# The third block's projections over 528 columns: meta tokens beside the tokens, keys and first values weights-stationary

## Chip, core and metric

The kernel runs on one core of a Trainium2 chip. The metric is device time in microseconds (us) from the start of the program to its end, the median of the runs shown. TensorE's granted clock has two levels, 1.2 and 2.4 GHz; a granted clock of 1.00 is the upper one.

## What is computed

Two blocks of one kind (layers 0 and 1) and then a block of another kind (the third block, `L2` in the code) work on 512 tokens of width 1024. The third block puts 16 learned meta tokens ahead of the 512, so that keys and values have 528 rows, and projects the normalised tokens to two kinds of queries, keys and values. Queries and keys are normalised per head of 64 and rotated:

```python
meta = jnp.broadcast_to(meta_tokens.astype(x.dtype)[None], (bsz, N_META, D_MODEL))
x = jnp.concatenate([meta, x], axis=1)
...
h = rms_norm(x, attn_norm_g[l])
proj = jnp.einsum('bld,de->ble', h, w_in[l])
qa, ka, va, qb, kb, vb = jnp.split(proj, splits, axis=-1)
qa = apply_rope_2(rms_norm(qa.reshape(bsz, length, A_HEADS, HEAD_DIM), a_q_norm_g[l]), ang_a)
ka = apply_rope_2(rms_norm(ka.reshape(bsz, length, A_KV_HEADS, HEAD_DIM), a_k_norm_g[l]), ang_a)
va = va.reshape(bsz, length, A_KV_HEADS, HEAD_DIM)
...
return x[:, N_META:]
```

Attention over `ka`, `va` and the differential attention over `kb`, `vb` follow, then an output projection and a feed-forward part. Only the 512 rows of the tokens are returned, so the meta tokens need keys and values alone, and no queries.

## The kernel before, in words

Activations lie transposed: 128 features to a partition row, `KT` = 8 tiles of features, 512 tokens along the free dimension. Every product of an activation and a weight is done as three matmuls (`product`, line 1759): both operands are split into a high and a low part (`h_hi`, `h_lo`, `w_hi`, `w_lo`), and high x low, low x high and high x high are added up in PSUM. One chunk of weights is 128 x 1024; SyncE (SP) loads the chunks in order into six slots, each when the chunk six places ahead has been used up (`w_used`), and GpSimd (POOL) splits each into its two parts. Nothing schedules the work but the order in which each engine's instructions are written down, and semaphores.

Four places matter here.

The first is `gemm_first` (line 1804). It follows a norm whose output comes in two halves of 256 tokens, eight feature tiles each; VectorE (DVE) finishes a tile of `h_lo` at line 1197 and counts `h_ready`. TensorE takes three chunks (four in the third block) side by side, half by half, and within a half tile by tile: for each feature tile `k` it waits for that tile and then does all chunks. Layer 1 calls it for `ik`, `iq0`, `iq1`, the third block for `qa0` to `qa3`.

The second is the run of key tiles (from line 2252): `ka0`, `kb0` to `kb3`. For each, 24 matmuls stream the 512 tokens through the weights; then `meta_keys` (line 2227) does 24 more with the 16 meta tokens as the stationary operand and the 128 weight columns streamed, into its own PSUM bank; then `head_sums_2` (line 2236) adds up squares of an earlier tile, one full-precision matmul over 512 columns.

The third is the values `va` (from line 2262): tokens are the stationary operand, four blocks of 128 tokens with 24 matmuls of 128 columns each; between the blocks stand two head sums and the five small transposes that turn the meta keys (`kmt`, line 2270); then 24 matmuls for the meta tokens' values (`vam`), the head sum of the meta keys, and at once the first block of `vb` (`values_in(0, ...)`), after which the scores begin (`scores_2`, line 2312 in the rows).

The fourth is the chain beside it. ScalarE (ACT) copies each finished tile from PSUM (`raw2`, line 1062), starts two DMAs that swap neighbouring rows (line 732), squares it (line 1067) and, when TensorE has summed the squares of the tile before, takes that tile's Ln and Exp (lines 752 and 753). DVE does the rotation of each tile in four instructions (`rope_2`, lines 1388 to 1405), using the swapped rows and the result of the Exp. The scores wait for all rotations (`rope_done`). There are 14 rows in this list of tiles, `R2_NAMES`: eight of queries, five of keys, and `mk`, the 80 columns of the meta keys.

Of the kernel before, what the change touches and what calls it, by code (L numbers as in the profile page):

```python
# [16 lines left out]
F32 = mybir.dt.float32  # L17
# [6 lines left out]
P = 128  # L24
D = 1024
T = 512
# [36 lines left out]
TM = T + META  # L63
L2 = LAYERS
GRID = 64
R2_NAMES = ("qa0", "qa1", "qa2", "qa3", "qb0", "qb1", "qb2", "qb3", "ka0", "kb0", "kb1", "kb2", "kb3", "mk")
# [48 lines left out]
def weight_plan():  # L115
# [36 lines left out]
    def second_mixer(l):  # L152
        for i, n in enumerate(R2_NAMES[:-1]):
            chunks.append((l, n))
            tile((l, n), i if i < 4 else (i - 4) % 3)
        tile((l, "mk"), 3)
# [83 lines left out]
def program(nc, wst, xin, pos, cst, vec, cst2, meta, gates, out):  # L240
    chunks, index, ready, bankof, seq, before = weight_plan()
    ctx = ExitStack()
    with ctx:
# [9 lines left out]
        h_hi = sbt("h_hi", 16, KT, T, dt=F32R)  # L253
        h_lo = sbt("h_lo", 32, KT, T, dt=F32R)
        w_raw = [sbt(f"w_raw{i}", 48 + 8 * i, 1024) for i in range(WSLOTS)]
        w_lo = [sbt(f"w_lo{i}", 48 + 8 * i, 1024, dt=F32R) for i in range(WSLOTS)]
        w_hi = [sbt(f"w_hi{i}", 52 + 8 * i, 1024, dt=F32R) for i in range(WSLOTS)]
        cos_t, sin_t = sbt("cos_t", 96, T), sbt("sin_t", 98, T)
        rstd = sbt("rstd", 100, T)
        kc = sbt("kc", 102, C_W)  # L260
        vecs = sbt("vecs", 106.28125, V_W)
        small = sbt("small", 106.625, 128)
        WK = 107.25
# [44 lines left out]
        hm_hi = sbt("hm_hi", WK + 99, KT, META, dt=F32R)  # L308
        hm_lo = sbt("hm_lo", WK + 99.5, KT, META, dt=F32R)
# [4 lines left out]
        raw2 = [sbt(f"raw2{i}", WK + 51 + 2 * i, T) for i in range(TURNS)]  # L314
        rsq2 = [sbt(f"rsq2{i}", WK + 63 + 2 * i, T) for i in range(2)]
        rrs2 = [sbt(f"rrs2{i}", WK + 67 + 2 * i, T) for i in range(2)]
        rt3, rt4 = sbt("rt3", WK + 71, T), sbt("rt4", WK + 73, T)
        rot2 = [sbt(f"rot2{i}", WK + 75 + 2 * i, T) for i in range(TURNS)]
        kmt = sbt("kmt", WK + 87, 5 * P)
# [4 lines left out]
        kept = [sbt(f"kept{i}", 96 + 2 * i, T) for i in range(KEPT)]  # L324
# [8 lines left out]
        def bank(b, lo=0, n=512):  # L333
            return ps[:, 512 * b + lo:512 * b + lo + n]

# [90 lines left out]
        kmt_ready = sem("kmt_ready")  # L426
        mk_ready = sem("mk_ready")
# [185 lines left out]
        def _(eng):  # L613
# [85 lines left out]
            def scaled_top(n, j):  # L699
# [8 lines left out]
                eng.activation(h_hi[:, j, :], x_sb[:, j, :], ACT.Copy, scale=vecs[:, g:g + 1]).then_inc(hi_ready, 1)  # L708
# [38 lines left out]
            def head_norm_2(r):  # L747
                w = 5 * META if R2_NAMES[r] == "mk" else T
                eng.wait_ge(rms_ready, Q0 + r + 1)
                if r >= 2:  # L750
                    eng.wait_ge(rope_done, R0 + r - 1)
                after(step(eng.activation(rrs2[r % 2][:, 0:w], bank(6 + r % 2, 0, w), ACT.Ln, scale=1.0 / AD, bias=eps)))
                eng.activation(rrs2[r % 2][:, 0:w], rrs2[r % 2][:, 0:w], ACT.Exp, scale=-0.5).then_inc(rrs_ready, 1)

            for l in range(LAYERS):
# [207 lines left out]
                def split_y(i):  # L963
# [4 lines left out]
                    eng.activation(h_hi[:, i, :], src, ACT.Copy).then_inc(ysp_hi, 1)  # L968
# [81 lines left out]
            for r in range(len(R2_NAMES)):  # L1050
                n = (L2, R2_NAMES[r])
                w = 5 * META if n[1] == "mk" else T
                if n[1] == "mk":
                    acc(n)
                    eng.activation(kmt[0:META, :], ps[0:META, 3 * 512:3 * 512 + 5 * P], ACT.Copy).then_inc(kmt_ready, 1)
                    eng.wait_ge(mk_ready, 1)
                    a = bank(5)
                else:
                    a = acc(n)
                if r >= TURNS:  # L1060
                    eng.wait_ge(rope_done, R0 + r - TURNS + 1)
                free(eng.activation(raw2[r % TURNS][:, 0:w], a[:, 0:w], ACT.Copy), n)
# [8 lines left out]

            free(eng.activation(va_sb[:, :, :].rearrange("p a b -> p (a b)"), acc((L2, "va")), ACT.Copy), (L2, "va"))
# [43 lines left out]
            def result(u):  # L1116
# [5 lines left out]
                if u < PAIRS_A:  # L1122
                    eng.activation(h_hi[:, u, :], bank(7), ACT.Copy).then_inc(ysp_hi, 1)
# [8 lines left out]
            def kept_split(u):  # L1132
                acc((L2, "vb3"))
                eng.wait_ge(y2_kept, u + 1)
                eng.activation(h_hi[:, u, :], kept[u][:, :], ACT.Copy).then_inc(ysp_hi, 1)
# [6 lines left out]
            def result_split(h):  # L1142
                eng.wait_ge(yb_ready, h + 1)
                eng.activation(h_hi[:, 4 + h, :], osb2[:, :], ACT.Copy).then_inc(ysp_hi, 1)
# [25 lines left out]
        def _(eng):  # L1170
# [63 lines left out]
            def scaled_rest(n, j):  # L1234
                g = V_NORM + 8 * n + j
                eng.wait_ge(hi_ready, tiles_before(n) + j + 1)
                eng.scalar_tensor_tensor(h_lo[:, j, :], x_sb[:, j, :], vecs[:, g:g + 1], h_hi[:, j, :].bitcast(F32),
# [115 lines left out]
            def meta_norm():  # L1353
# [9 lines left out]
                after(step(eng.tensor_copy(hm_hi[:, :, :], sqm[:, :, :])))  # L1363
                eng.tensor_tensor(hm_lo[:, :, :], sqm[:, :, :], hm_hi[:, :, :].bitcast(F32), ALU.subtract)\
# [7 lines left out]
            def rope_2(r):  # L1372
# [1211 lines left out]
```

## Time and profile before

| | us |
|---|---|
| median of three runs | 2254.21 |
| lowest and highest run | 2252.89, 2254.99 |
| span of the profiled execution | 2253.1 |
| TensorE busy | 2230.7 (99%) |
| GpSimd busy | 1484.0 (66%) |
| VectorE busy | 1034.2 (46%) |
| ScalarE busy | 618.9 (27%) |

The profile gives the profiled execution's time as its span alone, from the first to the last instruction. Busy shares are averages over all stages. A matmul's shown duration is longer than its share of the engine, because matmuls overlap; what one costs is the distance from its start to the start of the next. The third block begins near 1594 us of the span, its scores near 1705 us; layer 1 begins near 805 us.

### The profile page before, as it was taken

The page shows a single profiled execution, that of the slowest core. Times are in us where ns is not written, and L with a number is a line of the kernel's source. Part 1 is how long each engine was busy: PE and PEld are TensorE (multiplying, and loading weights), DVE is VectorE, ACT ScalarE, POOL GpSimd, SP SyncE. Part 2 cuts the span into 40 slices and gives each one's busy share as a digit, 9 for nine tenths or more (in the row PEclk, how much of TensorE's full clock was granted, in tenths as well). Part 3 has the DMA queues.
Part 4 walks back from the last instruction along what each step waited for, and adds up shares of the span by engine and source line. Part 5 has one row for each costly group of instructions (what it writes and reads, how often), then busy time and mean ns, then how long its engine had stood idle before and what let it go on. Part 6 is the DMA issues. An engine that isn't in the chain of part 4 may idle for free.

```text
span 2253.1 us, 33380 instructions
## 1 busy us (share of the span) xinstructions
PE 2230.7 (99%) x12339; PEld 1795.8 (80%) x12339; DVE 1034.2 (46%) x1567; ACT 618.9 (27%) x1103; POOL 1484.0 (66%) x1452
## 2 busy tenths in 40 slices
PE   8999999999999999999999999999999999999999
PEld 7777888888888897778788888888986568888887
DVE  6975745533331049759554333310484564333200
ACT  4335334221110033353342211110334553111100
POOL 6654876866766756549768677667593337776673
PEclk9999999999999999999999999999999999999999
DMA  5321344333333333223343333333330103323332
GB/s 188 105 75 57 114 122 140 103 100 96 93 101 95 95 119 103 75 60 110 122 142 102 103 93 99 97 94 93 127 113 11 38 1 109 97 93 101 95 94 84
DMA packets 69870, 217.53 MB, mean 97 GB/s; under 512 B 8448, under 2 KB 10752, under 8 KB 69632
## 3 DMA queue, kind: packets, MB, share of 16 engines
q1 hardware_dynamic: 54016, 188.41, 27.4%
q10 hardware_dynamic: 15744, 27.52, 3.4%
q8 instruction: 85, 1.39, 0.3%
q14 instruction: 25, 0.20, 0.0%
HBM read 195.93 MB, written 10.49 MB: 92 GB/s over the span
## 4 chain that ended last, share of the span: by engine, by line
PE 94%; DVE 3%; ACT 2%; issue 1%; ACTq 0%; DMA 0%; POOL 0%; DVEq 0%; POOLq 0%
PE ps L1765 83%; PE ps L2312 1%; PE ps L2038 1%; PE ps L2143 1%; PE ps L2067 1%; PE ps L2052 1%; PE ps L2367 1%; PE ps L1988 1%; PE ps L2334 1%; ACT pe L1095 1%; DVE small L1415 0%; PE ps L2241 0%; PE ps L2011 0%; DVE p_sb L1564 0%; PE ps L2172 0%
## 5 line engine op out<-in xcount | busy, mean ns | idle before, releaser
L562 POOL TENSOR_TENSOR w_lo<-w_raw,w_hi 128x512 fp32r<-128x512 f32 x700 | 958.0, 1369 | 58.4
L559 POOL TENSOR_SCALAR w_hi<-w_raw 128x512 fp32r<-128x512 f32 x700 | 505.0, 721 | 595.8 <-DMA w_raw<-wst 554.1
L1765 PE MATMUL ps<-h_hi,w_lo 128*128 128x512 f32 (+1 forms) x2056 | 804.6, 391 | 2.7 <-DVE h_lo L1229 2.5
L1765 PE MATMUL ps<-h_hi,w_hi 128*128 128x512 f32 (+1 forms) x2056 | 783.8, 381 | 0.0
L1765 PE MATMUL ps<-h_lo,w_hi 128*128 128x512 f32 (+1 forms) x2056 | 783.7, 381 | 0.0
L1765 PEld LDWEIGHTS ps<-h_hi,w_lo 128*128 128x128 f32 x2056 | 386.5, 188 | 100.3 <-issue 19.6
L1765 PEld LDWEIGHTS ps<-h_lo,w_hi 128*128 128x128 f32 x2056 | 386.7, 188 | 78.5 <-issue 7.4
L1765 PEld LDWEIGHTS ps<-h_hi,w_hi 128*128 128x128 f32 x2056 | 386.5, 188 | 75.1
L1765 PE MATMUL ps<-a_hi,w_lo 128*128 128x512 f32 (+1 forms) x572 | 213.7, 374 | 0.0
L1765 PE MATMUL ps<-a_hi,w_hi 128*128 128x512 f32 (+1 forms) x572 | 213.2, 373 | 0.0
L1765 PE MATMUL ps<-a_lo,w_hi 128*128 128x512 f32 (+1 forms) x572 | 213.2, 373 | 0.0
L1299 DVE TENSOR_TENSOR x_sb<-x_sb,ps 128x512 f32<-128x512 f32 x46 | 31.4, 687 | 323.7 <-PE ps L1765 323.7
L1341 DVE TENSOR_TENSOR ft<-fs,ps 128x512 f32<-128x512 f32 x66 | 45.4, 687 | 211.1 <-PE ps L1765 210.8
L740 ACT ACTIVATE a_hi<-ft 128x512 f32 x66 | 41.8, 633 | 312.6 <-DVE ft L1341 312.6
L1765 PEld LDWEIGHTS ps<-a_lo,w_hi 128*128 128x128 f32 x572 | 107.7, 188 | 19.1
L1765 PEld LDWEIGHTS ps<-a_hi,w_lo 128*128 128x128 f32 x572 | 107.7, 188 | 18.9
L1765 PEld LDWEIGHTS ps<-a_hi,w_hi 128*128 128x128 f32 x572 | 107.7, 188 | 18.8
L1336 DVE TENSOR_TENSOR fs<-ps,rstd 128x512 f32<-128x512 f32 x66 | 45.6, 692 | 163.5 <-PE ps L1765 163.2
L1345 DVE TENSOR_TENSOR a_lo<-ft,a_hi 128x512 f32 x66 | 87.2, 1321 | 60.8 <-ACT a_hi L740 60.8
L738 ACT ACTIVATE fs<-fs 128x512 f32<-128x512 f32 x66 | 41.8, 633 | 250.9 <-DVE fs L1336 250.9
L652 ACT ACTIVATE sqb<-x_sb 128x512 f32<-128x512 f32 (+1 forms) x37 | 22.5, 609 | 234.3 <-DVE x_sb L1299 222.0
L1765 PE MATMUL ps<-w_lo,h_hi 128*128 128x512 f32 (+1 forms) x192 | 76.9, 400 | 0.0
(305 smaller groups left out, 2517.2 us busy)
## 6 DMA issues: line engine op xcount, KB each, us to landing
w_raw<-wst SPq DMA_DIRECT2D x350, 512.0 KB, 3.6
rot<-raw ACTq DMA_DIRECT2D x70, 128.0 KB, 3.5
gates<-gt ACTq DMA_DIRECT2D x32, 256.0 KB, 4.3
stage<-gates ACTq DMA_DIRECT2D x32, 256.0 KB, 4.1
x_sb<-xin SPq DMA_DIRECT2D x8, 256.0 KB, 7.2
out<-x_sb SPq DMA_DIRECT2D x8, 256.0 KB, 4.4
kc<-cst ACTq DMA_DIRECT2D x1, 1056.0 KB, 5.1
kc<-cst SPq DMA_DIRECT2D x1, 417.0 KB, 8.5
```

What stands on the lines that cost most here:

```text
L559: eng.tensor_scalar(w_hi[s][:, part], w_raw[s][:, part], 1.0, 1.0, ALU.mult, ALU.mult)\
L562: eng.tensor_tensor(w_lo[s][:, part], w_raw[s][:, part], w_hi[s][:, part].bitcast(F32), ALU.subtract)\
L738: eng.activation(fs[s][:, :], fs[s][:, :], ACT.Silu).then_inc(silu_ready, 1)
L740: eng.activation(a_hi[:, bass.ds(r * 2 + s, 1), :].rearrange("p o t -> p (o t)"), ft[s][:, :], ACT.Copy)\
L1095: eng.activation(pe[u % 2][:, 2 * b + i, :], score_tile(u, i), ACT.Exp, bias=small[:, col:col + 1], accum_out=small[:, 16 + col:17 + col])\
L1299: eng.tensor_tensor(x_sb[:, i, :], x_sb[:, i, :], a, ALU.add).then_inc(x_new, 1)
L1336: eng.tensor_tensor(fs[s][:, :], bank(b), rstd[:, :], ALU.mult).then_inc(gs_ready, 1)
L1341: eng.tensor_tensor(ft[s][:, :], fs[s][:, :], bank(bankof[(l, f"u{s}")]), ALU.mult)\
L1345: eng.tensor_tensor(a_lo[:, i, :].rearrange("p o t -> p (o t)"), ft[s][:, :], a_hi[:, i, :].rearrange("p o t -> p (o t)").bitcast(F32), AL ...
L1765: m = eng.matmul(o, w, x, start=first and i == 0, stop=final and i == 2)
L1988: eng.matmul(bank(6 + i % 2), block, rsq[i % 2][:, :], start=True, stop=True).then_inc(rms_ready, 1)
L2038: eng.matmul(bank(SCORE_BANKS[b % 2][i], 0, NKEYS[b]), q_sb[rows, p, b * P:(b + 1) * P], k_sb[rows, p, 0:NKEYS[b]], start=True, stop=True) ...
```

## The change

The norm's output `h_hi`, `h_lo` becomes 528 columns wide; the normalised meta tokens, which had tiles of their own, are written to its last 16 columns. Each of the five key tiles, and `va`, is now computed with the weights stationary over all 528 columns, as two matmuls of 264 columns in two neighbouring PSUM banks (`wide_gemm`). With that `meta_keys`, the row `mk` and its small transposes go. `va`, which now comes out features first, is copied by ScalarE to `vat` and turned by TensorE with five transposes (four of 128 tokens and one of 16). The second half of `gemm_first` is written chunk by chunk instead of tile by tile, for both of its callers. Bank numbers change to make room for pairs: the key tiles alternate between banks 0, 1 and 2, 3, the head sums between 6, 7 and 4, 5. The buffers of the rotation become 528 wide. Elsewhere only the slice `0:T` of the wider tiles is written out.

```diff
-R2_NAMES = ("qa0", "qa1", "qa2", "qa3", "qb0", "qb1", "qb2", "qb3", "ka0", "kb0", "kb1", "kb2", "kb3", "mk")
+R2_NAMES = ("qa0", "qa1", "qa2", "qa3", "qb0", "qb1", "qb2", "qb3", "ka0", "kb0", "kb1", "kb2", "kb3")
...
+            tile((l, n), i % 4 if i < 8 else 2 * (i % 2))
         chunks.append((l, "va"))
-        tile((l, "va"), 0)
-        tile((l, "vam"), 1)
+        tile((l, "vaw"), 2)
+        tile((l, "va"), 0, False)
+        tile((l, "vam"), 1, False)
...
+        def wide(b):
+            return ps[:, 512 * b:512 * b + 1024].rearrange("p (n c) -> p n c", c=512)[:, :, 0:HW]
...
             def head_norm_2(r):
-                w = 5 * META if R2_NAMES[r] == "mk" else T
+                w = TM if R2_NAMES[r][0] == "k" else T
...
+                dst, src = (both(raw2[r % TURNS]), wide(bankof[n])) if w == TM else (raw2[r % TURNS][:, 0:T], a)
+                free(eng.activation(dst, src, ACT.Copy), n)
...
+            acc((L2, "vaw"))
+            free(eng.activation(both(vat), wide(bankof[(L2, "vaw")]), ACT.Copy), (L2, "vaw"))
             free(eng.activation(va_sb[:, :, :].rearrange("p a b -> p (a b)"), acc((L2, "va")), ACT.Copy), (L2, "va"))
...
-                for half in range(2):
+                for k in range(KT):
+                    if k == 4:
+                        mean_square(n, 1)
+                    eng.wait_ge(h_ready, tiles_before(n) + k + 1)
+                    for r in range(len(cs)):
+                        part(r, k, 0)
+                    if k == 3 and len(names) > 3:
+                        cs.append(chunk(names[3]))
+                        for j in range(k + 1):
+                            part(3, j, 0)
+                for r in range(len(cs)):
                     for k in range(KT):
-                        if half == 0 and k == 4:
-                            mean_square(n, 1)
-                        eng.wait_ge(h_ready, tiles_before(n) + 8 * half + k + 1)
-                        for r in range(len(cs)):
-                            part(r, k, half)
-                        if half == 0 and k == 3 and len(names) > 3:
-                            cs.append(chunk(names[3]))
-                            for j in range(k + 1):
-                                part(3, j, half)
+                        eng.wait_ge(h_ready, tiles_before(n) + KT + k + 1)
+                        part(r, k, 1)
...
+            def wide_gemm(name, tile, behind={}):
+                c = chunk(name)
+                b = bankof[tile]
+                begin(tile)
                 for k in range(KT):
+                    for i in range(2):
+                        cols = slice(HW * i, HW * i + HW)
+                        m = product(bank(b + i, 0, HW), *weights(c, k), h_hi[:, k, cols], h_lo[:, k, cols],
+                                    k == 0, k == KT - 1)
+                    if k in behind:
+                        head_sums_2(behind[k])
                 m.then_inc(w_used, 1)
...
+                if R2_NAMES[r][0] == "k":
+                    eng.matmul(bank(b, 0, HW), block, rsq2[r % 2][:, 0:HW], start=True, stop=True)
+                    m = eng.matmul(bank(b + 1, 0, HW), block, rsq2[r % 2][:, HW:TM], start=True, stop=True)
+                else:
+                    m = eng.matmul(bank(b), block, rsq2[r % 2][:, 0:T], start=True, stop=True)
...
+            eng.wait_ge(hm_ready, 1)
+            for i, n in enumerate(R2_NAMES[8:]):
+                if i < 2:
+                    taken(eng, (L2, f"qb{2 * i + 1}"))
+                wide_gemm((L2, n), (L2, n))
                 head_sums_2(6 + i)
-            name = (L2, "va")
-            c, o = chunk(name), begin(name)
+            wide_gemm((L2, "va"), (L2, "vaw"), {1: 11, 5: 12})
+            taken(eng, (L2, "vaw"))
+            begin((L2, "va"))
             for t in range(TB):
...
+                m = eng.transpose(bank(0, t * P, P), vat[:, t * P:(t + 1) * P], ident)
+            m.then_inc(acc_ready, 1)
             begin((L2, "vam"))
...
+            eng.transpose(bank(1, 0, P)[0:META, :], vat[:, T:TM], ident).then_inc(acc_ready, 1)
```

How the order of instructions moves is shown at three places of TensorE's list. In these rows `h_hi_50` and `h_lo_51` are the norm's output, `w_lo3_61`, `w_hi3_67` and the like are the parts of one weight slot (the digit before the underscore is the slot), and a row ends with the semaphores that it waits for.

The second half of `gemm_first` in layer 1, before:

```order
L1765 MATMUL ps<-h_hi_50,w_lo3_61 128x256 [waits h_ready]
L1765 MATMUL ps<-h_lo_51,w_hi3_67 128x256
L1765 MATMUL ps<-h_hi_50,w_hi3_67 128x256
L1765 MATMUL ps<-h_hi_50,w_lo4_62 128x256
L1765 MATMUL ps<-h_lo_51,w_hi4_68 128x256
L1765 MATMUL ps<-h_hi_50,w_hi4_68 128x256
L1765 MATMUL ps<-h_hi_50,w_lo5_63 128x256
L1765 MATMUL ps<-h_lo_51,w_hi5_69 128x256
L1765 MATMUL ps<-h_hi_50,w_hi5_69 128x256
L1765 MATMUL ps<-h_hi_50,w_lo3_61 128x256 [waits h_ready]
```

The same half with the change, from the last two feature tiles of its first chunk:

```order
L1758 MATMUL ps<-h_hi_50,w_lo3_61 128x256 [waits h_ready]
L1758 MATMUL ps<-h_lo_51,w_hi3_67 128x256
L1758 MATMUL ps<-h_hi_50,w_hi3_67 128x256
L1758 MATMUL ps<-h_hi_50,w_lo3_61 128x256 [waits h_ready]
L1758 MATMUL ps<-h_lo_51,w_hi3_67 128x256
L1758 MATMUL ps<-h_hi_50,w_hi3_67 128x256
L1758 MATMUL ps<-h_hi_50,w_lo4_62 128x256 [waits h_ready]
L1758 MATMUL ps<-h_lo_51,w_hi4_68 128x256
L1758 MATMUL ps<-h_hi_50,w_hi4_68 128x256
```

Before, each wait for a feature tile was followed by the nine matmuls of three chunks; now slot 3 takes all eight tiles, with a wait ahead of every three matmuls, before slot 4 begins.

The end of a key tile, the head sum and the beginning of the next key tile, before:

```order
L1765 MATMUL ps<-w_lo5_63,hm_hi_144 16x128
L1765 MATMUL ps<-w_hi5_69,hm_lo_145 16x128
L1765 MATMUL ps<-w_hi5_69,hm_hi_144 16x128
L2241 MATMUL ps<-rsq21_160,kc_73 128x512 [waits rrs_ready,rsq_ready]
L1765 MATMUL ps<-h_hi_50,w_lo0_58 128x512 [waits acc_free2,w_ready]
L1765 MATMUL ps<-h_lo_51,w_hi0_64 128x512
L1765 MATMUL ps<-h_hi_50,w_hi0_64 128x512
```

and with the change:

```order
L1758 MATMUL ps<-h_hi_50,w_lo4_62 128x264
L1758 MATMUL ps<-h_lo_51,w_hi4_68 128x264
L1758 MATMUL ps<-h_hi_50,w_hi4_68 128x264
L2244 MATMUL ps<-rsq20_158,kc_73 128x264 [waits rrs_ready,rsq_ready]
L2245 MATMUL ps<-rsq20_158,kc_73 128x264
L1758 MATMUL ps<-h_hi_50,w_lo5_63 128x264 [waits acc_free2,w_ready]
L1758 MATMUL ps<-h_lo_51,w_hi5_69 128x264
L1758 MATMUL ps<-h_hi_50,w_hi5_69 128x264
```

The 24 short matmuls of the meta tokens are gone from the end of the tile, and the head sum of a key row is two matmuls.

The way from `va` to `vb`, before (around the small transposes of line 2270):

```order
L1765 MATMUL ps<-w_lo1_59,h_hi_50 128x128
L1765 MATMUL ps<-w_hi1_65,h_lo_51 128x128
L1765 MATMUL ps<-w_hi1_65,h_hi_50 128x128
L2270 MATMUL ps<-kc_73,kmt_171 128x16 [waits kmt_ready]
L2270 MATMUL ps<-kc_73,kmt_171 128x16 x4
L1765 MATMUL ps<-w_lo1_59,h_hi_50 128x128
L1765 MATMUL ps<-w_hi1_65,h_lo_51 128x128
L1765 MATMUL ps<-w_hi1_65,h_hi_50 128x128
```

and with the change, from the last matmuls of `va` to the first of `vb`:

```order
L1758 MATMUL ps<-h_hi_50,w_lo1_59 128x264
L1758 MATMUL ps<-h_lo_51,w_hi1_65 128x264
L1758 MATMUL ps<-h_hi_50,w_hi1_65 128x264
L2265 MATMUL ps<-kc_73,vat_151 128x128 [waits acc_free0,acc_free2]
L2265 MATMUL ps<-kc_73,vat_151 128x128 x3
L2268 MATMUL ps<-kc_73,vat_151 16x128 [waits acc_free1]
L1758 MATMUL ps<-w_lo2_60,h_hi_50 128x512 [waits w_ready,rrs_ready,acc_free4]
L1758 MATMUL ps<-w_hi2_66,h_lo_51 128x512
L1758 MATMUL ps<-w_hi2_66,h_hi_50 128x512
```

The transposes now stand directly behind the last matmul of `va` and wait (`acc_free2`) for ScalarE's copy of it, and `vb` stands behind them.

## Rows read from the trace of the kernel before

**Rows 1.** The profile page: engine totals, granted clock, chain by engine, one weight-load group.

```profile
PE 2230.7 (99%) x12339; PEld 1795.8 (80%) x12339; DVE 1034.2 (46%) x1567; ACT 618.9 (27%) x1103; POOL 1484.0 (66%) x1452
PEclk9999999999999999999999999999999999999999
PE 94%; DVE 3%; ACT 2%; issue 1%; ACTq 0%; DMA 0%; POOL 0%; DVEq 0%; POOLq 0%
L1765 PEld LDWEIGHTS ps<-h_hi,w_lo 128*128 128x128 f32 x2056 | 386.5, 188 | 100.3 <-issue 19.6
```

**Rows 2.** The chain in order of time, third block: start us, us, what.

```profile
1600.13 0.43 PE ps L1889 x2
1600.57 0.43 PE ps L1891 x2
...
1645.75 6.92 PE ps L1765 x48
1652.67 0.91 PE ps L2241 x2
...
1684.72 2.63 PE ps L1765 x24
...
1699.33 5.49 PE ps L1765 x24
1704.82 1.24 PE ps L2312 x8
...
1722.18 1.02 PE ps L2334 x8
```

**Rows 3.** Timeline of TensorE: start us, us, instruction.

```profile
814.59 0.28 PE L1765 MATMUL ps<-h_hi,w_lo 128*128 128x256 f32 x1
...
823.23 0.40 PE L1765 MATMUL ps<-h_hi,w_lo 128*128 128x512 f32 x1
...
1618.11 0.40 PE L1765 MATMUL ps<-h_hi,w_lo 128*128 128x512 f32 x1
...
1653.65 0.39 PE L1765 MATMUL ps<-h_lo,w_hi 128*128 128x512 f32 x1
...
1658.63 0.39 PE L1765 MATMUL ps<-h_hi,w_hi 128*128 128x512 f32 x1
...
1684.73 0.27 PE L1765 MATMUL ps<-w_hi,h_hi 128*128 128x128 f32 x1
...
1687.08 0.27 PE L1765 MATMUL ps<-w_hi,h_hi 128*128 128x128 f32 x1
```

**Rows 4.** Timeline of VectorE: last tiles of the norm's second half, layer 1, third block.

```profile
819.00 0.99 DVE L1197 TENSOR_TENSOR h_lo<-htb,h_hi 128x256 fp32r<-128x256 f32 x2
...
1608.67 0.42 DVE L1197 TENSOR_TENSOR h_lo<-htb,h_hi 128x256 fp32r<-128x256 f32 x1
```

**Rows 5.** Timeline of ScalarE in the third block.

```profile
1617.23 0.60 ACT L1062 ACTIVATE raw<-ps 128x512 f32<-128x512 f32 x1 [8.59 <-PE ps L1765]
...
1624.63 0.69 ACT L752 ACTIVATE rrs<-ps,small 128x512 f32<-128x512 f32 x1 [2.44 <-PE ps L2241]
...
1684.76 0.69 ACT L752 ACTIVATE rrs<-ps,small 128x512 f32<-128x512 f32 x1 [4.12 <-PE ps L2241]
1685.48 0.63 ACT L753 ACTIVATE rrs<-rrs 128x512 f32<-128x512 f32 x1
```

**Rows 6.** Timeline of VectorE: rotations of `qa0`, `qb3` and the meta keys end.

```profile
1628.29 0.99 DVE L1405 SCALAR_TENSOR_TENSOR qab<-rt,rrs 128x512 f32<-128x512 f32 x1
...
1666.31 0.98 DVE L1405 SCALAR_TENSOR_TENSOR qab<-rt,rrs 128x512 f32<-128x512 f32 x1
...
1700.10 0.24 DVE L1400 TENSOR_TENSOR kab<-rt,rrs 128x80 f32<-128x80 f32 x1 [0.32 <-ACT rrs L753]
```

**Rows 7.** Busy us (and instructions) by stretch: PE, PEld, DVE, ACT, POOL; PEclk, DMA share.

```profile
0.00:10.00 10.00, 5.14 (x24) 5.14 (x25) 3.21 (x10) 4.06 (x9) 0.20 (x4) 1.00 0.77 253
```

**Rows 8.** Timeline of GpSimd: the split of chunk `wo1`, waiting for its load.

```profile
1703.06 0.62 POOL L559 TENSOR_SCALAR w_hi<-w_raw 128x512 fp32r<-128x512 f32 x1 [9.77 <-DMA w_raw<-wst]
```

More of the change, by code:

```diff
@@ L252, in program @@
         x_sb = sbt("x_sb", 0, KT, T)
[L253 to L263, printed above, removed]
+        h_hi = sbt("h_hi", 16, KT, TM, dt=F32R)
+        h_lo = sbt("h_lo", 32.5, KT, TM, dt=F32R)
+        w_raw = [sbt(f"w_raw{i}", 49 + 8 * i, 1024) for i in range(WSLOTS)]
+        w_lo = [sbt(f"w_lo{i}", 49 + 8 * i, 1024, dt=F32R) for i in range(WSLOTS)]
+        w_hi = [sbt(f"w_hi{i}", 53 + 8 * i, 1024, dt=F32R) for i in range(WSLOTS)]
+        cos_t, sin_t = sbt("cos_t", 97, T), sbt("sin_t", 99, T)
+        rstd = sbt("rstd", 101, T)
+        kc = sbt("kc", 103, C_W)
+        vecs = sbt("vecs", 106.78125, V_W)
+        small = sbt("small", 107.125, 128)
+        WK = 107.625
         f_sb = sbt("f_sb", WK, 4, T)
@@ L313, in program @@
         vb_sb, vbm_sb = sbt("vb_sb", WK + 41, 4, T), sbt("vbm_sb", WK + 49, T)
[L314 to L319, printed above, removed]
+        vat = sbt("vat", WK + 35.5, TM)
+        raw2 = [sbt(f"raw2{i}", WK + 51 + 2.0625 * i, TM) for i in range(TURNS)]
+        rsq2 = [sbt(f"rsq2{i}", WK + 63.375 + 2.0625 * i, TM) for i in range(2)]
+        rrs2 = [sbt(f"rrs2{i}", WK + 67.5 + 2.0625 * i, TM) for i in range(2)]
+        rt3, rt4 = sbt("rt3", WK + 71.625, TM), sbt("rt4", WK + 73.6875, TM)
+        rot2 = [sbt(f"rot2{i}", WK + 75.75 + 2.0625 * i, TM) for i in range(TURNS)]
         pe = [sbt(f"pe{i}", WK + 51 + 17 * i, 8, TM) for i in range(2)]
@@ L323, in program @@
         vmz = sbt("vmz", WK + 40.5, P)
-        kept = [sbt(f"kept{i}", 96 + 2 * i, T) for i in range(KEPT)]
+        kept = [sbt(f"kept{i}", 97 + 2 * i, T) for i in range(KEPT)]
         osq2, ors2 = sbt("osq2", WK, T), sbt("ors2", WK + 2, T)
@@ L334, in bank, with both, sums_bank @@
             return ps[:, 512 * b + lo:512 * b + lo + n]
+        def wide(b):
+            return ps[:, 512 * b:512 * b + 1024].rearrange("p (n c) -> p n c", c=512)[:, :, 0:HW]
+        def both(t):
+            return t[:, :].rearrange("p (n c) -> p n c", c=HW)
+        def sums_bank(r):
+            return 6 - 2 * (r % 2)
         def relu_tile(u, nk):
@@ L1798, in gemm_last_output @@
                         chunk((L2, "wo7"))
-                    m = product(o, *weights(c, k), h_hi[:, k, :], h_lo[:, k, :], k == 0, k == KT - 1)
+                    m = product(o, *weights(c, k), h_hi[:, k, 0:T], h_lo[:, k, 0:T], k == 0, k == KT - 1)
                     if k < KT - 1:
@@ L1917, in wide @@
                             eng.wait_ge(w_ready, r * 24 + (2 * c + 2))
-                        m = product(bank(b), *weights(c, k), h_hi[:, k, :], h_lo[:, k, :], k == 0, k == KT - 1)
+                        m = product(bank(b), *weights(c, k), h_hi[:, k, 0:T], h_lo[:, k, 0:T], k == 0, k == KT - 1)
                     m.then_inc(w_used, 1)
@@ L1928, in ffn @@
                     for c, o in zip(cs, os):
-                        m = product(o, *weights(c, k), h_hi[:, k, :], h_lo[:, k, :], k == 0, k == KT - 1)
+                        m = product(o, *weights(c, k), h_hi[:, k, 0:T], h_lo[:, k, 0:T], k == 0, k == KT - 1)
                         if k == KT - 1:
@@ L2013, in _ @@
                     for k in BEHIND_PAIR.get(j, ()):
-                        m = product(q3, *weights(c, k), h_hi[:, k, :], h_lo[:, k, :], k == 0, k == KT - 1)
+                        m = product(q3, *weights(c, k), h_hi[:, k, 0:T], h_lo[:, k, 0:T], k == 0, k == KT - 1)
                         if k == KT - 1:
@@ L2078, in fill @@
                         c = half_chunk(name) if k < KT // 2 else chunk(name)
-                        m = product(o, *weights(c, k), h_hi[:, k, :], h_lo[:, k, :], k == 0, k == KT - 1)
+                        m = product(o, *weights(c, k), h_hi[:, k, 0:T], h_lo[:, k, 0:T], k == 0, k == KT - 1)
                         if k == KT - 1:
@@ L2197, in projected @@
                         eng.wait_ge(ysp_lo, 8 * l + kk + 1)
-                        m = product(o, *weights(c, kk), h_hi[:, kk, :], h_lo[:, kk, :], k == 0, k == 3)
+                        m = product(o, *weights(c, kk), h_hi[:, kk, 0:T], h_lo[:, kk, 0:T], k == 0, k == 3)
                     m.then_inc(w_used if half else acc_ready, 1)
@@ L2240, in head_sums_2 @@
                     eng.wait_ge(rrs_ready, Q0 + r - 1)
-                eng.matmul(bank(6 + r % 2, 0, w), block, rsq2[r % 2][:, 0:w], start=True, stop=True)\
-                   .then_inc(rms_ready, 1)
+                b = sums_bank(r)
+                if R2_NAMES[r][0] == "k":
[3 more added lines that the diff above has]
+                    m = eng.matmul(bank(b), block, rsq2[r % 2][:, 0:T], start=True, stop=True)
+                m.then_inc(rms_ready, 1)
             for i in range(4):
@@ L2399, in early @@
                 eng.wait_ge(ysp_lo, 8 * L2 + SPLIT_ORDER.index(k) + 1)
-                m = product(bank(5), *weights(c, k), h_hi[:, k, :], h_lo[:, k, :], k == 3, k == 2)
+                m = product(bank(5), *weights(c, k), h_hi[:, k, 0:T], h_lo[:, k, 0:T], k == 3, k == 2)
                 if k == 2:
@@ L2438, in _ @@
                 for i in range(4):
-                    m = product(bank(i), *weights(cs[i], k), h_hi[:, k, :], h_lo[:, k, :], k == 4, k == KT - 1)
+                    m = product(bank(i), *weights(cs[i], k), h_hi[:, k, 0:T], h_lo[:, k, 0:T], k == 4, k == KT - 1)
                     if k == KT - 1:
```

120 lines of the change are left out of this document (33 added, 87 removed).

## Prediction, made before the changed kernel ran

> **What bounds the kernel now.** I read the page first: TensorE is busy 99% of the span at a granted clock of 1.00 (the upper level, 2.4 GHz) in every slice, and the chain that ended last is 94% TensorE [rows 1]. So a microsecond that TensorE spends more or less in a stage should come out in the total, unless another engine steps in there. To see whether one does, I read the chain in order of time over the start of the third block [rows 2]: key tiles, `va` and `vb` follow each other on TensorE without a break, and the scores start at 1704.82. Then the timelines: on TensorE I read distances between starts, since shown durations overlap [rows 3]; on VectorE and ScalarE I look for work that would be late if TensorE came earlier [rows 4 to 6].
>
> **Prices.** From the distances [rows 3]: a matmul of 256 columns with new weights each time takes (823.23 - 814.59) / 72 = 0.1200 us, one of 512 columns (1658.63 - 1653.65) / 22 = 0.2264. A straight line between them gives 0.1233 for 264 columns. The 128-column matmuls of `va` take (1687.08 - 1684.73) / 21 = 0.1119, hardly less than those of 256, so short matmuls here pay for something other than their columns; 264 columns lie on the upper side of that, next to a row at 256, and I take 0.1233. The bounds are 0.120 and the 0.188 that a weight load is shown to last [rows 1].
>
> **Key tiles.** Before, five tiles with their head sums take 1684.72 - 1645.75 = 38.97 us [rows 2]. Now each is 48 matmuls of 264 columns, 48 x 0.1233 = 5.92, and a head sum. A head sum over 512 columns is 0.91, two full-precision matmuls over 256 columns are 0.43 each [rows 2]; scaled to 264 that is 2 x 0.43 x 264/256 = 0.89 for a pair. I take 0.89 for all five: 5 x (5.92 + 0.89) = 34.05. Gain 4.9 us.
>
> **`va`.** Before, from its first matmul to the first of `vb`: 1699.33 - 1684.72 = 14.61 us [rows 2], with two head sums, the small transposes and the meta values in it. Now: 5.92 for 48 matmuls, 2 x 0.89 for the head sums, then a new wait, since the transposes stand behind ScalarE's copy of the whole result and `vb` stands behind the transposes. The copy of 512 columns takes 0.60 [rows 5], so 528 take 0.62; with the two handovers I estimate 0.70. It can't be shorter than 0.6, and is longer if ScalarE is late: before the copy it has the Ln and Exp of the last key row, 0.69 + 0.63 [rows 5], which can start when the second head sum is done, and TensorE then still has two of eight feature tiles to do, 12 x 0.1233 = 1.48. So ScalarE is free just in time; were its Ln and Exp not covered at all, the wait would be about 2.0. Transposes: eight of 128 x 128 take 1.02 [rows 2], 0.1275 each, so five take 0.64. Together 5.92 + 1.78 + 0.70 + 0.64 = 9.04. Gain 5.6 us, from 4.3 with the late copy to 5.7.
>
> For a transpose the Trainium skill (TensorE: Matmul & The Clock Gate, Part 4: PE-mode transpose) gives some 275 ns inside a kernel; with that the five would take 1.4 us and the gain be 0.7 us less. The row of this kernel decides for 0.1275.
>
> **`gemm_first`, third block.** The half's 96 matmuls begin at 1618.11 - 96 x 0.12 = 1606.59 [rows 3]. Chunk by chunk, the first chunk reaches feature tile 7 after 7 x 0.36 = 2.52 us, at 1609.11; VectorE has finished that tile at 1608.67 + 0.42 = 1609.09 [rows 4]. It just fits: 0, at most 0.1 lost.
>
> **`gemm_first`, layer 1.** This is the same code with three chunks, not the third block, and here it does not fit. The half begins at 814.59 [rows 3], so tile 7 would be wanted at 814.59 + 2.52 = 817.11, but VectorE finishes the last two tiles of `h_lo` at 819.00 + 0.99 = 819.99 [rows 4]. Before, nine matmuls followed each tile, TensorE reached tile 7 at 814.59 + 7 x 1.08 = 822.15, and no wait showed. Now TensorE gives up its place behind each tile to wait for the next; queued behind that wait are the other two chunks, ready long ago for their early tiles. It gets tile 7 at 819.99, finishes the first chunk 0.36 later and does two whole chunks of 24 matmuls after that: 819.99 + 0.36 + 5.76 = 826.11, with a handover 826.15, against 823.23. Loss 2.9 us, between 2.8 and 3.3. The chunks `ik` and `iq0` are released or finished at other times, but the engines that use them have idle time there; TensorE does not.
>
> **What is late next.** The scores wait for all rotations. They would now start at 1704.8 - 10.5 = 1694.3 on this trace's clock. The first rotation ends at 1628.29 + 0.99 = 1629.28, and seven later `qb3` ends at 1666.31 + 0.98 = 1667.29 [rows 6]: 5.43 us each. `qa0` now comes out earlier, some 7 us (it ends at 1609.5, where ScalarE took it at 1617.23 [rows 5]), but its Exp still hangs on the head sum behind `qb0`, so its Ln stays at 1624.63 [rows 5], its Exp ends about 1626, and its rotation at about 1627. Twelve more, seven of queries at 5.43 and five of keys at 5.43 x 528/512 = 5.60, end by 1627 + 38.0 + 28.0 = 1693.0; the fourteenth, of the meta keys, is gone (it ended at 1700.34 [rows 6]). That leaves 1.3 us, and more if GpSimd's weight splitting, beside which the slow pace was seen, pauses. The weights hide: chunk `wo1`, which GpSimd must split before its part in the softmax, was waiting for its load until 1703.06 [rows 8]; that load is triggered by the release of `va`, now 0.70 + 0.64 + 5.49 = 6.8 us before the scores. The wider copies, squares and rotations cost 3% of instructions that lie beside TensorE's work; I cost them at nothing while the rotations keep that lead.
>
> **Sum.** -4.9 - 5.6 + 0.05 + 2.9 = -7.5 us. The span of 2253.1 becomes 2245.6; the median of the runs, 2254.2, lies 1.1 above that span, and I carry that over: 2246.7.
>
> **Rivals.**
> *A, the stop in layer 1 costs nothing.* Then only the third block counts: 2254.2 - 10.4 = 2243.8. It needs VectorE to be sooner with the norm's tiles, or another engine to bound layer 1 behind it. Against it: the tiles come from VectorE and ScalarE in turn, which nothing in the change touches, and TensorE is the chain's 94%. Chance 0.11.
>
> *B, the rotations set the start of the scores.* If the first rotation ends as before at 1629.28 and the others keep the pace beside weight splitting, the last ends at 1629.28 + 66.0 = 1695.3, 1 us after TensorE gets there; at 5.75 us for each of twelve it is 4 us. With 1 to 4 us lost: 2247.7 to 2250.7. For it: only 1.3 us of lead; against: splitting runs out of loaded weights near the end. Chance 0.15.
>
> *C, the weight loads of the 264-column matmuls show (slower).* Place: 6 x 48 = 288 matmuls that now load weights every 264 columns, where 512 columns stood behind a load before. At the 0.188 a load lasts [rows 1], each costs 0.065 more: 18.6 us, 2246.7 + 18.6 = 2265.3, slower than before. It turns the sign when a matmul takes over 0.1233 + 7.5 / 288 = 0.149. Against it stands the 0.1200 at 256 columns with new weights at each [rows 3]. Chance 0.03.
>
> *D, TensorE's clock falls in the new stops.* In the first ten microseconds TensorE is busy only 5.14 of 10 us and the granted clock is 1.00 [rows 7]; the stop in layer 1 leaves it busy about 2.9 us of 5.5, spread over it. If the clock did fall to 1.2 GHz behind both stops, the two chunks of 5.76 and the `vb` block of 5.49 [rows 2] would take twice as long: 11.2 us, 2258. The Trainium skill (TensorE: Matmul & The Clock Gate, HAM oscillation) says that idle gaps between bursts of matmuls bring the clock to its lower level; by that rule this is the case to expect wherever the stops count as such gaps. The trace shows no fall so far. Chance 0.03.
>
> *E, the change does nothing measurable in sum*: a late copy before the transposes (1.3 us), a longer stop in layer 1 (0.4) and B together leave 2 to 4 us of gain. Chance 0.08.
>
> **How the numbers follow.** The forecast, 2246.7 within about 1.3 us, gets 0.60. About 0.2%, 4.5 us, is what a measurement of this kernel can tell from no change, so faster means under 2249.7: forecast, A, and two thirds of B, 0.60 + 0.11 + 0.10 = 0.81. Slower (over 2258.7) is C and part of D: 0.04. The rest is 0.15. The range takes in A at the low end and most of B and E at the high one: 2243.5 to 2251.0.
>
> **What would show it.** Right: 48 matmuls per key tile 0.123 us apart, 6.8 us from one head sum to the next; 9.0 us from `va` to `vb` with one gap of about 0.7 before the transposes; in layer 1 TensorE waiting for `h_lo` in the second half, and its first 512-column matmul about 2.9 us later after that half's start than now; in the third block no such wait; DVE's last rotation before the first score. Wrong: a distance over 0.13 at 264 columns, a granted clock under 1.00 behind a stop, scores released by VectorE, or layer 1 without a wait.

## The result, and the profile after

| | before | after |
|---|---|---|
| median of four runs, us | 2254.38 | 2280.68 |
| lowest and highest | 2252.89, 2254.99 | 2280.20, 2281.07 |
| span of the profiled execution, us | 2253.1 | 2279.2 |

The changed kernel is slower: the ratio is 1.012, with a 95% interval of 1.0108 to 1.0131. The prediction was 2246.7 us; the time lies 29.7 us above its range. The profile page of the changed kernel, against [rows 1]:

```profile
PE 2257.0 (99%) x12275; PEld 1792.4 (79%) x12275; DVE 1019.5 (45%) x1561; ACT 618.6 (27%) x1099; POOL 1481.3 (65%) x1452
PEclk9999999999999999999999999999999999999999
PE 95%; DVE 3%; ACT 2%; issue 0%; DMA 0%; ACTq 0%; POOL 0%; DVEq 0%; POOLq 0%
```

TensorE does 64 instructions fewer and is busy 26.3 us longer, as much as the total grew, at a mean granted clock of 1.00, the upper level. Its idle time is what it was (2253.1 - 2230.7 = 22.4 us before, 2279.2 - 2257.0 = 22.2 after), so in sum the loss is not a wait. The stage that was rewritten is not where it lies either. The chain in order of time over the third block (start us, us, what), against [rows 2]:

```profile
1628.55 0.43 PE ps L1887 x2
1628.98 22.82 PE ps L1758 x168
...
1667.52 5.57 PE ps L1758 x24
...
1693.95 5.80 PE ps L1758 x48
1699.75 0.45 PE ps L2244 x2
1700.20 0.45 PE ps L2245 x2
1700.64 5.80 PE ps L1758 x48
...
1707.34 1.45 PE ps L1758 x12
...
1713.47 1.48 PE ps L1758 x12
1714.95 0.02 issue
1714.97 0.62 ACT vat L1078
1715.59 0.04 issue
1715.64 0.66 PE ps L2265 x4
1716.29 0.11 PE ps L2268
1716.40 5.56 PE ps L1758 x24
1721.96 1.24 PE ps L2304 x8
```

From the end of the norm's mean square to the first score it was 1704.82 - (1600.57 + 0.43) = 103.82 us; now it is 1721.96 - 1628.98 = 92.98. This stage gained 10.8 us. But it begins 28 us later, and one row points to why: the 24 matmuls of the first `vb` block took 5.49 us [rows 2] and take 5.56 now. The timeline of TensorE over the 24 of a `qb` tile (start us, us, instruction), against the 512-column stretch in [rows 3]:

```profile
1667.59 0.40 PE L1758 MATMUL ps<-h_lo,w_hi 128*128 128x512 f32 x1
...
1672.69 0.39 PE L1758 MATMUL ps<-h_hi,w_hi 128*128 128x512 f32 x1
```

The second is 22 starts behind the first, 5.10 / 22 = 0.2318 us apart, against 0.2264. Nothing in the diff touches what these instructions compute. The groups by line and shape show that it is not this place alone. Before (what it does, shapes and count, busy us, mean ns of one):

```profile
L1765 PE MATMUL ps<-h_lo,w_hi 128*128 128x512 f32 x1896 | 738.5, 389 | 0.0
L1765 PE MATMUL ps<-a_hi,w_hi 128*128 128x512 f32 x484 | 188.3, 389 | 0.0
L1765 PE MATMUL ps<-m_lo,w_hi 128*128 128x512 f32 x128 | 49.8, 389 | 0.0
```

The same groups of the changed kernel:

```profile
L1758 PE MATMUL ps<-h_lo,w_hi 128*128 128x512 f32 x1856 | 733.5, 395 | 0.0
L1758 PE MATMUL ps<-a_hi,w_hi 128*128 128x512 f32 x484 | 191.0, 395 | 0.0
L1758 PE MATMUL ps<-m_lo,w_hi 128*128 128x512 f32 x128 | 50.5, 394 | 0.0
```

All 512-column matmuls of the split products lasted longer, in layers 0 and 1 as well, even those of `a` (the feed-forward's inner activations) and `m` (what the output projection `wo` reads in these layers), whose code is the same. From all start times in the trace, a matmul of `a` or `m` follows the last one after 226.7 ns on average before and 232.5 after. With 5568 such matmuls of `h`, 1452 of `a` and 384 of `m`, 4 to 6 ns each come to 30 to 44 us. The stretches agree: the span grew by 26.1 us although this stage became 10.8 shorter and the stop in layer 1, below, added only 3.0, so some 34 us were added outside these two places.

What the full diff does to all of them is in its table of tiles, which the excerpt in "The change" leaves out: rows of `h_hi` and `h_lo` are 2112 bytes apart instead of 2048, the weight slots begin at 49 KB instead of 48, and the work area with `a` and `m` at 107.625 KB instead of 107.25.

### The profile page after: what moved, and what is told of

Read it like the earlier page. It is cut to its first block, busy times and chain, and to the rows that moved or that the text cites. A ratio compares the mean times of both kernels' runs of the same rounds, so it can differ in the third digit from the quotient of the medians.

```text
span 2279.2 us, 33236 instructions
## 1 busy us (share of the span) xinstructions
PE 2257.0 (99%) x12275; PEld 1792.4 (79%) x12275; DVE 1019.5 (45%) x1561; ACT 618.6 (27%) x1099; POOL 1481.3 (65%) x1452
## 4 chain that ended last, share of the span: by engine, by line
PE 95%; DVE 3%; ACT 2%; issue 0%; DMA 0%; ACTq 0%; POOL 0%; DVEq 0%; POOLq 0%
PE ps L1758 84%; PE ps L2304 1%; PE ps L2034 1%; PE ps L2048 1%; PE ps L2139 1%; PE ps L2063 1%; PE ps L2359 1%; PE ps L1984 1%; PE ps L2326 1%; ACT pe L1102 1%; DVE small L1408 0%; PE ps L2007 0%; PE ps L2168 0%; PE ps L2184 0%; ACT p_sb L857 0%
## 5 line engine op out<-in xcount | busy, mean ns | idle before, releaser
L568 POOL TENSOR_SCALAR w_hi<-w_raw 128x512 fp32r<-128x512 f32 x700 | 497.6, 711 | 622.6 <-DMA w_raw<-wst 581.2
L1758 PE MATMUL ps<-h_hi,w_lo 128*128 128x512 f32 (+2 forms) x2112 | 823.2, 390 | 4.3 <-DVE h_lo L1236 2.8
L1758 PE MATMUL ps<-h_lo,w_hi 128*128 128x512 f32 (+2 forms) x2112 | 805.7, 381 | 0.0
L1758 PE MATMUL ps<-h_hi,w_hi 128*128 128x512 f32 (+2 forms) x2112 | 802.3, 380 | 0.0
L1758 PEld LDWEIGHTS ps<-h_hi,w_lo 128*128 128x128 f32 x2112 | 396.9, 188 | 111.7 <-issue 20.1
L1758 PEld LDWEIGHTS ps<-h_lo,w_hi 128*128 128x128 f32 x2112 | 396.6, 188 | 84.9 <-issue 6.9
L1758 PEld LDWEIGHTS ps<-h_hi,w_hi 128*128 128x128 f32 x2112 | 397.2, 188 | 79.3
L1352 DVE TENSOR_TENSOR a_lo<-ft,a_hi 128x512 f32 x66 | 78.2, 1184 | 60.8 <-ACT a_hi L749 60.8
L1758 PE MATMUL ps<-w_lo,h_hi 128*128 128x512 f32 (+1 forms) x168 | 70.9, 422 | 0.0
```

The costliest lines, as they stand in the source:

```text
L568: eng.tensor_scalar(w_hi[s][:, part], w_raw[s][:, part], 1.0, 1.0, ALU.mult, ALU.mult)\
L1352: eng.tensor_tensor(a_lo[:, i, :].rearrange("p o t -> p (o t)"), ft[s][:, :], a_hi[:, i, :].rearrange("p o t -> p (o t)").bitcast(F32), AL ...
L1758: m = eng.matmul(o, w, x, start=first and i == 0, stop=final and i == 2)
```

## Experiments

Theories: **addresses** (the place of the operands in SBUF sets the spacing) against **computation** (the new tiles, waits and copies slow the others); then, within addresses, the streamed tile, the weight slots, or the distance between the two. Each run is given with its ratio to the kernel before, timed beside it (medians of before: 2253.34 beside runs 1 to 4, 2253.67 beside 5, 7, 8 and 9, 2253.98 beside 6). The spacings are means over all start times in the trace.

### 1. The old work with the new layout

```diff
-h_hi = sbt("h_hi", 16, KT, T, dt=F32R)
-h_lo = sbt("h_lo", 32, KT, T, dt=F32R)
+h_hi = sbt("h_hi", 16, KT, TM, dt=F32R)[:, :, 0:T]
+h_lo = sbt("h_lo", 32.5, KT, TM, dt=F32R)[:, :, 0:T]
...
-WK = 107.25
+WK = 107.625
```

(and weight slots and constants 1 KB higher, as in the change.)

> The kernel before, computing as it did, with every SBUF tile where the changed kernel has it (h_hi and h_lo 528 columns apart, weight slots 1 KB higher, the work area at 107.625 KB). Theory 'addresses' (the 512-column matmuls got 5.8 ns slower each because of where their operands lie in SBUF): spacing 232.5 ns in place of 226.7 for about 5700 matmuls of h, 1450 of a and 384 of m; 7500 x 5.8 ns = 43 us at most, and by the slower spacing of h as seen in the changed kernel (4 ns on average) some 34; total 2285 to 2297. Theory 'computation' (the new tiles, waits or copies of the changed kernel slow the others): 2254, spacing 226.7.

Measured: 2288.65 us, ratio 1.0157 (1.0140 to 1.0174); `a` and `m` 232.5 ns apart. The old computation is slower than the changed kernel as soon as `h`, the weight slots and the work area lie where the change puts them (the third block's own buffers keep their old places within the work area). Computation as the cause is out.

### 2. The work area alone

```diff
-WK = 107.25
+WK = 107.625
```

> The kernel before with the work area alone moved, from 107.25 to 107.625 KB (384 bytes), so that a_hi, a_lo, m_hi and m_lo move and h and the weights stay. Theory 'moving operand' (the address of the tile that a matmul streams, by itself or against that of the weights, sets its spacing): a and m at 232.5 ns, h at 226.7; 1836 x 5.8 ns = 10.6 us, total 2265. Theory 'weight slots' (the slots' move by 1 KB did it): no change, 2254.4.

Measured: 2265.17 us, ratio 1.0052 (1.0035 to 1.0069). The groups by line and shape of this run:

```profile
L1765 PE MATMUL ps<-h_lo,w_hi 128*128 128x512 f32 x1896 | 738.5, 389 | 0.0
L1765 PE MATMUL ps<-a_hi,w_hi 128*128 128x512 f32 x484 | 191.1, 395 | 0.0
L1765 PE MATMUL ps<-m_lo,w_hi 128*128 128x512 f32 x128 | 50.5, 395 | 0.0
```

One number of the program, 384 bytes, costs 11.8 us, and of these groups exactly those whose tiles it moves are slow. The weight slots stood still.

### 3. `h` alone, by 128 bytes

```diff
-h_hi = sbt("h_hi", 16, KT, T, dt=F32R)
-h_lo = sbt("h_lo", 32, KT, T, dt=F32R)
+h_hi = sbt("h_hi", 16.125, KT, T, dt=F32R)
+h_lo = sbt("h_lo", 32.125, KT, T, dt=F32R)
```

(weight slots and everything behind them 256 bytes higher.)

> The kernel before with h_hi and h_lo moved by 128 bytes, and the weight slots and all that lies behind them by 256 bytes. Theory 'moving operand, period of 256 bytes': h at about 232.5 ns, a and m at 226.7; 5700 x 5.8 ns = 33 us, total 2287. If a move of 256 bytes matters as well, a and m are slow too: 2297. Theory 'weight slots': h and a and m alike, all slow (2297) or none (2254).

Measured: 2283.22 us, ratio 1.0131 (1.0114 to 1.0148). Now `h` is slow and the others are not:

```profile
L1765 PE MATMUL ps<-h_lo,w_hi 128*128 128x512 f32 x1896 | 748.0, 395 | 0.0
L1765 PE MATMUL ps<-a_hi,w_hi 128*128 128x512 f32 x484 | 188.3, 389 | 0.0
```

29.9 us over 5688 matmuls is 5.3 ns each, a little under the 5.8 expected. The move of 256 bytes did nothing.

### 4. Everything by 128 bytes

```diff
-origin = -(-nc.sbuf_base // 32) * 32
+origin = -(-nc.sbuf_base // 32) * 32 + 128
```

> The kernel before with every SBUF tile moved by the same 128 bytes. If the spacing hangs on the address of an operand itself (modulo 256), all 512-column matmuls of h, a and m are slow: 7500 x 5.8 ns = 43 us, total 2297. If it hangs on the distance between the streamed tile and the weights, nothing changes: 2254.4.

Measured: 2253.21 us, ratio 1.0001 (0.9991 to 1.0011); 226.3 to 227.0 ns apart for `a` and `m`. So the address by itself does not matter; the distance between tiles does. In run 2 the streamed tiles `a_hi` and `a_lo` kept their distance to each other and were slow, which leaves their distance to tiles that stood still; that these are the weights is tested in run 5.

### 5. The weight slots by 64 bytes

```diff
-w_lo = [sbt(f"w_lo{i}", 48 + 8 * i, 1024, dt=F32R) for i in range(WSLOTS)]
+w_lo = [sbt(f"w_lo{i}", 48.0625 + 8 * i, 1024, dt=F32R) for i in range(WSLOTS)]
```

(`w_raw` and `w_hi` likewise; what lies behind them 256 bytes higher.)

> The kernel before with the weight slots moved by 64 bytes, and what lies behind them by 256, so that h, a and m all stand 64 bytes off a multiple of 256 from the weights. If every odd distance costs the same 5.8 ns: 7500 x 5.8 ns = 43 us, total 2297, though here no streamed tile has been moved against the start of the memory except by 256. If 64 bytes cost less than 128: between 2254 and 2297. If only 128 bytes matter, or if the weights' place plays no part: 2254.

Measured: 2297.11 us, ratio 1.0191 (1.0176 to 1.0207); 233.0 to 233.6 ns apart for `a` and `m`, `h` slow too. 64 bytes cost no less than 128, and this move of the weights alone (what lies behind them moved by 256 bytes, which did nothing in run 3) costs the whole 43 us.

### 6. `h_lo` alone, by 128 bytes

```diff
-h_lo = sbt("h_lo", 32, KT, T, dt=F32R)
+h_lo = sbt("h_lo", 32.125, KT, T, dt=F32R)
```

(weight slots and everything behind them 256 bytes higher.)

> The kernel before with h_lo alone moved by 128 bytes against the weights and h_hi (weight slots and all behind them moved by 256 bytes). One in three of the 512-column matmuls of h streams h_lo. If a misplaced tile slows only the matmul that streams it: some 1900 x 5.8 ns = 11 us, total 2265, and one of the three spacings of h at some 232 ns, the others at 227. If it slows its neighbours as well: up to 2287, as with h_hi and h_lo both moved.

Measured: 2283.31 us, ratio 1.0135 (1.0118 to 1.0152), as much as with both moved. One misplaced matmul in three slows its neighbours: the commonest spacings within a trio are 236, 234 and 230 ns instead of 227 each. `h_lo` has moved against `h_hi` too here; in run 3 the two kept their distance and the cost was the same.

### 7. The changed kernel, work area at 107.75 KB

```diff
-WK = 107.625
+WK = 107.75
```

> The changed kernel with the work area alone moved by another 128 bytes, from 107.625 to 107.75 KB, which puts a_hi, a_lo, m_hi and m_lo back at a multiple of 256 bytes from the weight slots; h keeps its 2112-byte rows. Theory 'distance to the weights, period 256 bytes': a and m return to 226.7 ns, h stays slow; 1836 x 5.8 ns = 10.6 us less than the changed kernel's 2280.7, total 2270. Rival 'the higher the area lies, or the new computation beside it, the slower': no gain, 2280 or more.

Measured: 2269.96 us, ratio 1.0072 (1.0056 to 1.0087), 10.7 us less than the changed kernel (10.0 when each is set against the kernel before timed beside it). Its groups:

```profile
L1758 PE MATMUL ps<-h_lo,w_hi 128*128 128x512 f32 x1856 | 733.7, 395 | 0.0
L1758 PE MATMUL ps<-a_hi,w_hi 128*128 128x512 f32 x484 | 188.3, 389 | 0.0
```

128 bytes more of padding give back what `a` and `m` lost.

### 8. Two views of `h`

```diff
-h_hi = sbt("h_hi", 16, KT, TM, dt=F32R)
-h_lo = sbt("h_lo", 32.5, KT, TM, dt=F32R)
+h_hi, hw_hi = sbt("h_hi", 16, KT, T, dt=F32R), sbt("hw_hi", 16, KT, TM, dt=F32R)
+h_lo, hw_lo = sbt("h_lo", 32.5, KT, T, dt=F32R), sbt("hw_lo", 32.5, KT, TM, dt=F32R)
...
-WK = 107.625
+WK = 107.75
```

(`hw_hi` and `hw_lo` in the third block's norm, `gemm_first`, `qb`, `wide_gemm` and `vb`.)

> The changed kernel with the work area at 107.75 KB and h_hi and h_lo laid out in two ways over the same bytes: rows of 512 columns (2048 bytes) everywhere but in the third block's projections, which alone use rows of 528. Theory 'the prediction's terms are right and the distance to the weights was the one thing left out': about 2247 (the 2246.7 predicted, and some 0.5 for the 96 matmuls of qb that still stream from rows of 528). Rival 'the new tiles, the stop in layer 1 or ScalarE's wider work cost several us more than predicted': 2250 or more.

Measured: 2246.45 us (2244.45 to 2246.69), ratio 0.9965 (0.9951 to 0.9978). The groups of `h` (in rows of 512 again) and `a`:

```profile
L1763 PE MATMUL ps<-h_lo,w_hi 128*128 128x512 f32 x1824 | 710.3, 389 | 0.0
L1763 PE MATMUL ps<-a_hi,w_hi 128*128 128x512 f32 x484 | 188.3, 389 | 0.0
```

That is 23.5 us less than run 7, from `h` alone. In run 5 a matmul cost 5.8 ns more (43.4 us over 7524); with rows of 2112 bytes, 64 more than a multiple of 256, one row in four still fits, so an estimate is 3/4 x 5568 x 5.8 ns = 24.2 us. That the fitting row is free of the cost is not shown: in the changed kernel's trace its three spacings are 226, 236 and 228 ns on average. With the tiles in place the change makes the kernel faster, by 7.2 us where the prediction summed to 7.5.

### 9. And layer 1 tile by tile again

```diff
-                for r in range(len(cs)):
-                    for k in range(KT):
-                        eng.wait_ge(h_ready, tiles_before(n) + KT + k + 1)
-                        part(r, k, 1)
+                steps = [(r, k) for r in range(len(cs)) for k in range(KT)]
+                if n < 2 * L2:
+                    steps = [(r, k) for k in range(KT) for r in range(len(cs))]
+                for r, k in steps:
+                    eng.wait_ge(h_ready, tiles_before(n) + KT + k + 1)
+                    part(r, k, 1)
```

> As the kernel with two views, and the second half of the norm's first projections goes feature tile by feature tile again in layer 1 (chunk by chunk in the third block alone). Theory 'the stop in layer 1 costs 2.9 us and lies on the path': 2.9 us under the kernel with two views, about 2244. Rival 'another engine sets the pace there and the stop costs nothing': the same as with two views.

Measured: 2243.64 us (2242.60 to 2244.49), ratio 0.9954 (0.9940 to 0.9967): 2.8 us under run 8, and 10 us under the kernel before. The chain of run 8 in layer 1 goes through ScalarE and VectorE:

```profile
808.27 0.45 PE ps L1892 x2
808.72 0.02 issue
808.74 0.48 ACT rstd L705
...
817.36 0.35 DVE h_lo L1209
817.70 0.04 issue
817.75 17.86 PE ps L1763 x102
```

and in run 9 it stays on TensorE behind the mean square:

```profile
808.35 0.43 PE ps L1894 x2
808.78 23.86 PE ps L1763 x156
```

To the end of that last piece it is 817.75 + 17.86 - 808.72 = 26.89 us in run 8 and 23.86 in run 9: 3.0 us.

## Why the prediction was wrong, step by step

**The step that failed** is the sum itself. "-4.9 - 5.6 + 0.05 + 2.9 = -7.5 us" holds for a kernel in which every other instruction costs what it did. The prediction took 0.2264 us for a 512-column matmul [rows 3] as a property of the instruction, and had no term for the tiles that the diff moves: it put their move at nothing without a reason. That price hangs on where the operands lie. Some 7400 matmuls pay 4 to 6 ns more; runs 7 and 8 size it at 10.0 us for `a` and `m` (against the kernel before beside each) and 23.5 for `h`, 33.5 together. With run 8's gain of 7.2 that is the 26.3 measured, but only because the three differences share their ends. The check that does not is run 1: there the layout alone, under the old computation, costs 35.3 us. The full diff showed which tiles move and by how much, the rows 64 bytes longer and the 384 bytes in the work area's base; what that costs stands in no row that the prediction read.

**The gains came as said.** Key tiles: the five with their head sums take 1707.34 - 1673.95 = 33.39 us, a gain of 5.6 where 4.9 was forecast:

```profile
1673.95 5.79 PE ps L1758 x48
1679.74 0.86 PE ps L2247 x2
```

The 48 matmuls take 5.80 us, 0.1208 each; 0.1233 was taken, from a straight line between 256 and 512 columns, and was too dear. A tile with its head sum takes 6.69 (1700.64 - 1693.95) where 6.81 was forecast. `va` to `vb`: 1716.40 - 1707.34 = 9.06 against 9.04, with a wait of 0.02 + 0.62 + 0.04 = 0.68 for ScalarE's copy (0.70). The five transposes take 0.66 + 0.11 = 0.77, where 0.64 was forecast. The prediction read the figure of the Trainium skill (TensorE: Matmul & The Clock Gate, Part 4: PE-mode transpose), some 275 ns, as a price, by which an estimate for the five is 1.4 us; here each of the four of 128 tokens is shown with a duration of 273 ns, which agrees with the page, but they overlap and cost 0.165 each, so the row of this kernel was the better guide. That run 8 lands within 0.3 us of 2246.7 is in part luck: key tiles 0.7 us cheaper than forecast, and the third block's own 512-column matmuls, which still read rows of 528 there, dearer (the first block of `vb` takes 5.56 us, not 5.49).

**`gemm_first`.** In the third block no wait shows: one piece of 168 matmuls runs from the mean square on. In layer 1 the stop is there. The end of the mean square in the chain before,

```profile
810.01 0.43 PE ps L1891 x2
810.44 23.86 PE ps L1765 x156
```

and after:

```profile
822.81 0.45 PE ps L1887 x2
823.26 0.02 issue
```

From there to the first 512-column matmul [rows 3] it was 823.23 - 810.44 = 12.79 us. Now TensorE waits for VectorE ahead of six of the eight feature tiles, as here (its timeline), and the chain is back on it only behind the seventh `h_lo` tile (the eighth costs another short wait):

```profile
831.48 0.38 PE L1758 MATMUL ps<-h_hi,w_lo 128*128 128x256 f32 x1 [0.24 <-DVE h_lo L1204]
```

```profile
832.30 0.04 issue
832.34 17.99 PE ps L1758 x102
```

TensorE's timeline has the first 512-column matmul at:

```profile
839.04 0.39 PE L1758 MATMUL ps<-h_hi,w_lo 128*128 128x512 f32 x1
```

From 823.26 that is 15.78. The loss is 3.0; forecast was 2.9, and run 9 gives 2.8. Rival A, that the stop costs nothing, is wrong.

**The rotations were not late** (rival B). VectorE's timeline, last rotation:

```profile
1717.36 0.71 DVE L1396 TENSOR_TENSOR kab<-rt,rrs 128x528 f32<-128x528 f32 x1
```

It ends at 1718.07, 3.9 us ahead of the first score at 1721.96; 1.3 was forecast. The queries kept the pace of 5.43 us, but the five key tiles took (1718.07 - 1692.87) / 5 = 5.04 each, from the end of the last query's rotation, where 5.60 was forecast.

**The other rivals.** C expected a slower kernel from the weight loads of the 264-column matmuls. Slower it is, but not by them: they stand 0.1208 us apart. D wanted a lower clock behind the stops. The page's digit 9 says only 90% or more; the stretches of the changed kernel's trace with the stop in layer 1 and right behind it show a granted clock of 1.00, the upper level (start:end us, length, busy us of TensorE, its weight loads, VectorE, ScalarE, GpSimd, then the clock and two figures on DMA):

```profile
823.00:832.40 9.40, 8.02 (x57) 6.77 (x55) 7.83 (x15) 4.23 (x11) 3.70 (x4) 1.00 0.00 0
832.40:846.00 13.60, 13.60 (x85) 12.13 (x86) 6.72 (x10) 3.48 (x6) 12.42 (x13) 1.00 0.59 186
```

So does the stretch around the wait before the transposes, 1714.90 to 1722.00. The fall that the prediction took from the Trainium skill (TensorE: Matmul & The Clock Gate, HAM oscillation) did not come with these stops. E, little in sum, is what none of the runs shows once the tiles lie well. No rival in the list was that the price changes of instructions whose code the diff leaves alone.

## What to carry to other kernels

When a change lengthens a tile or moves a base, look at the instructions that read the moved tiles, everywhere in the program, before costing the part that was rewritten: here some 2% on each of 7400 matmuls outweighed a clean gain in one stage. The sign of it is a group by line whose mean moved (389 to 395 ns) although its code did not. Before blaming a new algorithm, run the old one with the new layout; that one run separated the two here.

## What the runs showed of the hardware

Back-to-back 512-column matmuls with new weights each time stand 226.7 ns apart (`a`, `m`; 227.2 for `h`; means without the distances in which TensorE paused) when the streamed tile's start is a multiple of 256 bytes from the weight slot's (an odd multiple for `a` in the kernel before, even ones for `h`), and 232 to 234 when it is 64 or 128 bytes off such a multiple (runs 2, 3, 5). Moving both together by 128 bytes changes nothing (run 4). One misplaced tile in three costs almost as much as three in three (runs 3 and 6). The roles can be the other way round: the 504 matmuls that stream 512 columns of a weight slot against a piece of `h` went from 228.3 ns to 231.8 in the changed kernel.

Shorter matmuls did not get slower: with 256 columns those of `h` stand 119.9 ns apart before, 118.2 in the changed kernel and 116.3 in run 5. The full-precision head sum over 512 columns takes 0.86 us before and in run 2, where its streamed tile moved by 384 bytes against its weights. Which read the distance acts on (a matmul's own weights or the next one's), whether offsets under 64 bytes matter at 512 columns, and whether there is a longer period was not tried, so why the distance matters stays open.
